# The output projection by groups of token tiles, with kept weights and an early residual load

## The reference

```python
D_MODEL, D_FF, SEQ, DEC_BATCH, DEC_SEQ = 1024, 2816, 512, 8, 8

def trunk_layer(x, ...):
    z = rmsnorm(x, g_mix_pre)
    q, kc, vc, ks, vs, kw, vw, g_nsa, u, g_mrg = mixer_inputs(z, w_in)
    o_attn, win_state = attend(q, g_nsa, kc, vc, ks, vs, kw, vw)
    o_conv, conv_state = conformer_conv(u, conv_hist, conv_w, conv_b, conv_ln_g, conv_ln_b)
    h = (g_mrg[:, :, 0] * (o_attn @ w_attn_out) + g_mrg[:, :, 1] * (o_conv @ w_conv_out)) @ w_out
    x = x + rmsnorm(h, g_mix_post)
    f, ffn_state = conv_ffn(rmsnorm(x, g_ffn_pre), ffn_hist, w_up, ffn_conv_w, ffn_conv_b, w_down)
    x = x + rmsnorm(f, g_ffn_post)
    return x, kv_rows, win_state, conv_state, ffn_state
```

## Time and profile before

| | us |
|---|---|
| median of 3 executions | 1005.52 (1005.27 to 1006.03) |
| the profiled execution | 1006.05 |
| its span, first to last instruction | 1004.4 |
| PE busy in it | 950.4 (95%) |
| DVE busy | 575.2 (57%) |
| ACT busy | 399.6 (40%) |
| POOL busy | 208.4 (21%) |

### The profile page before, as it was taken

How to read it: one execution, slowest core, us unless ns; L and a number is a source line. 1 busy time by engine, 2 the same in 40 slices (tenths; PEclk the granted TensorE clock), 3 DMA queues, 4 the chain that set the end, 5 groups by cost and what they waited for, 6 DMA issues and landing times.

```text
span 1004.4 us, 17775 instructions
## 1 busy us (share of the span) xinstructions
PE 950.4 (95%) x6757; PEld 859.9 (86%) x6757; DVE 575.2 (57%) x1083; ACT 399.6 (40%) x734; POOL 208.4 (21%) x274
## 2 busy tenths in 40 slices
PE   4999999996999999899995999999999999999995
PEld 2899999996888878799774999999999997777774
DVE  4448688997565664567146466666666664113114
ACT  6211162644354434522136355555555552312112
POOL 6443242444232323022100011111111111000000
PEclk9999999997999999999995899999999999999998
DMA  7655532331100001122720222222222222131212
GB/s 215 148 178 187 128 87 78 95 85 43 51 23 2 23 22 39 47 63 85 213 84 0 63 84 84 84 84 84 84 84 84 84 84 84 63 98 65 84 63 95
DMA packets 110753, 84.05 MB, mean 84 GB/s; under 512 B 12962, under 2 KB 97834, under 8 KB 110632
## 3 DMA queue, kind: packets, MB, share of 16 engines
q1 hardware_dynamic: 104368, 65.64, 22.7%
q0 software_dynamic: 3904, 14.66, 5.2%
q10 hardware_dynamic: 2426, 2.98, 1.0%
HBM read 78.19 MB, written 7.18 MB: 85 GB/s over the span
## 4 chain that ended last, share of the span: by engine, by line
PE 88%; DVE 3%; ACT 3%; issue 2%; DMA 2%; POOL 1%; POOLq 0%; ACTq 0%; DVEq 0%
PE ps L1466 24%; PE ps L1467 24%; PE ps L1468 24%; PE ps L1498 2%; PE ps L1750 2%; PE ps L1727 2%; PE ps L1533 2%; DMA page<-in_state_kv_win_dram 2%; PE ps L1687 1%; DVE yc L1146 1%; PE ps L1690 1%; PE ps L1584 1%; PE ps L1693 1%; PE ps L1746 1%; POOL page L595 1%
## 5 line engine op out<-in xcount | busy, mean ns | idle before, releaser
L1466 PE MATMUL ps<-zh,wh 128*128 128x288 f32 (+1 forms) x1264 | 383.1, 303 | 2.1 <-DVE zl L1399 2.0
L1467 PE MATMUL ps<-zl,wh 128*128 128x288 f32 (+1 forms) x1264 | 374.4, 296 | 0.0
L1468 PE MATMUL ps<-zh,wl 128*128 128x288 f32 (+1 forms) x1264 | 374.4, 296 | 0.0
L1466 PEld LDWEIGHTS ps<-zh,wh 128*128 128x128 f32 (+1 forms) x1264 | 238.1, 188 | 4.4 <-issue 2.7
L1467 PEld LDWEIGHTS ps<-zl,wh 128*128 128x128 f32 (+1 forms) x1264 | 238.3, 189 | 0.5
L1468 PEld LDWEIGHTS ps<-zh,wl 128*128 128x128 f32 (+1 forms) x1264 | 237.9, 188 | 0.5
L1077 DVE TENSOR_TENSOR wl<-raw,wh 128x1024 fp32r<-128x1024 f32 (+1 forms) x73 | 95.4, 1306 | 203.9 <-ACT wh L734 203.7
L734 ACT CAST wh<-raw 128x1024 fp32r<-128x1024 f32 (+1 forms) x73 | 76.0, 1041 | 314.0 <-PE ps L1468 299.0
L1146 DVE SCALAR_TENSOR_TENSOR yc<-ext,par,yc 128x512 f32<-128x512 f32 (+1 forms) x180 | 115.9, 712 | 0.0
L1034 ACT CAST wh<-raw 128x1024 fp32r<-128x1024 f32 x44 | 46.1, 1049 | 139.4 <-PE ps L1468 139.4
L695 POOL TENSOR_TENSOR hs<-cv 128x512 f32<-128x512 f32 x22 | 28.5, 1297 | 325.2 <-DVE cv L1432 325.2
(11 more groups left out here) (260 smaller groups left out, 1324.9 us busy)
## 6 DMA issues: line engine op xcount, KB each, us to landing
raw<-in_w_up_dram SPq DMA_DIRECT2D x44, 512.0 KB, 3.8
raw<-in_w_in_dram SPq DMA_DIRECT2D x30, 512.0 KB, 3.9
raw<-in_w_down_dram SPq DMA_DIRECT2D x22, 512.0 KB, 3.6
page<-in_cache_kv_dram POOLq DMA_DIRECT2D x16, 256.0 KB, 3.0
raw<-in_w_out_dram SPq DMA_DIRECT2D x8, 512.0 KB, 3.5
x<-in_x_prompt_dram SPq DMA_DIRECT2D x4, 512.0 KB, 5.4
page<-in_state_kv_win_dram POOLq DMA_DIRECT2D x16, 128.0 KB, 3.0
raw<-in_w_in_dram SPq DMA_DIRECT2D x8, 256.0 KB, 3.5
```

The costliest lines, as they stand in the source:

```text
L1466: nc.tensor.matmul(out, ah, bh, start=start, stop=False)
L1467: nc.tensor.matmul(out, ah, bl, start=False, stop=False)
L1468: return nc.tensor.matmul(out, al, bh, start=False, stop=stop)
```

## The change

It touches the stretch from the merge to the first turn of `w_up`.

- `w_out` is computed by groups of token tiles: tiles 0, 1 and 2 together over all eight slots, then tile 3 over all eight, then tile 4. For that the eight slots are kept: slots 0 and 1 in the ring, 2 to 7 in places of their own (`wo1` to `wo4`), so that their high parts no longer wait for PE. The order of the slots is now by channel pair and then by half.
- A tile's norm, residual and second norm are made per tile with 1024 columns at a time (`square_out`, `scaled_out`, `add_out`, `square_x1`, `norm_x1`). `norm_x1` multiplies by `gffn`, a broadcast copy of `g_ffn_pre`, so the split into `z2` is a plain copy and subtraction.
- Each tile is transposed on its own (`turn_z2`), between the matmuls of the tiles behind it. `z2` is laid out by halves of 288 rows, and the first turn of `w_up` is taken out of the loop: both tiles' first halves, then the last transposes, then the second halves.
- POOL issues the loads of `x1` and `gffn` at the start of the merge, ahead of its adds, and `gpost` and `sf` after the merge.

```diff
@@ SP
-            for half in range(2):
-                for kc in range(KT // 2):
-                    s = S_OUT + half * (KT // 2) + kc
+            for kc in range(KT // 2):
+                for half in range(2):
+                    s = S_OUT + 2 * kc + half
                     ring_free(s)
@@ POOL
+            pool.wait_ge(c_step, 2 * CT)
+            pool.wait_ge(m_attn, 1)
+            for i in range(TT):
+                src = x_prompt[0, i * P:(i + 1) * P, :] if i < 4 else xs_v
+                pool.dma_start(x1[0:ROWS[i], i, :], src).then_inc(x1_in, 16)
+            pool.dma_start(gffn[:, :], g_ffn_pre[0].partition_broadcast(P)).then_inc(gf_in, 16)
+
             for m in range(KT):
                 pool.wait_ge(m_mul, 2 * m + 2)
...
@@ ACT
-            for kc in range(KT // 2):
-                hi(S_OUT + kc + 2)
+            for st in range(2, 8):
+                s = S_OUT + st
+                act.wait_ge(raw_in[s % 2], raw_value(s))
+                act.wait_ge(slot_used, S_MRG)
+                nc.scalar.copy(out_w(st)[0], raw[:, s % 2, :]).then_inc(hi_done, 1)
...
+            def z2_high(n):
+
+                i, src, high, _ = z2_piece(n)
+                act.wait_ge(z2_full, i + 1)
+                if n < 3:
+                    act.wait_ge(slot_used, S_OUT + 4)
+                else:
+                    act.wait_ge(o_tile, TT)
+                if n == 3:
+                    act.wait_ge(z2_ok, 3)
+                nc.scalar.copy(high, src).then_inc(z2_hi, 1)
+
+            for t in range(6):
+                if t < 3:
+                    square_out(t)
+                if 1 <= t < 4:
+                    root_out(t - 1)
+                if 2 <= t < 5:
+                    square_x1(t - 2)
                 if t >= 3:
...
+                    root_x1(t - 3)
+            square_out(3)
+            root_out(3)
+            square_x1(3)
+            root_x1(3)
+            for n in range(3):
+                z2_high(n)
+            hi(S_UP)
             hi(S_UP + 1)
+            square_out(4)
+            z2_high(3)
+            root_out(4)
+            z2_high(4)
+            square_x1(4)
+            root_x1(4)
+            z2_high(5)
@@ DVE
+            scaled_out(3)
+            dve.wait_ge(sf_t, 1)
...
+            add_out(3)
+            mean_x1(3)
+            norm_x1(3)
+            for n in range(3):
+                z2_low(n)
+            lo(S_UP)
             lo(S_UP + 1)
+            scaled_out(4)
+            z2_low(3)
+            add_out(4)
+            z2_low(4)
+            mean_x1(4)
+            norm_x1(4)
+            z2_low(5)
@@ PE
+            for kc in range(KT // 2):
+                pe.wait_ge(m_ok, 2 * kc + 2 + AHEAD)
+                for half in range(2):
+                    pe.wait_ge(lo_done, S_OUT + 2 * kc + half + 1)
+                    for i in range(3):
+                        if kc == 0 and i == 2:
+                            pe.wait_ge(m_mul, 2 * KT)
+                        mm = out_mm(i, kc, half)
+                        if kc == KT // 2 - 1 and half == 1:
+                            mm.then_inc(o_tile, 1)
+            for kc in range(KT // 2):
+                for half in range(2):
+                    mm = out_mm(3, kc, half)
+            mm.then_inc(o_tile, 1)
             pe.wait_ge(sf_in, 16)
+            pe.wait_ge(o_ev, 2)
             for t in range(2 * FT):
...
+            turn_z2(0)
+            pe.wait_ge(o_ev, 3)
+            for kc in range(KT // 2):
+                for half in range(2):
+                    mm = out_mm(4, kc, half, kc in (1, 2))
+                if kc == 0:
+                    pe.wait_ge(sf_ok, 1)
+                    turn_z2(1)
+                if kc == 1:
+                    pe.wait_ge(o_ev, 4)
+                    turn_z2(2)
+            mm.then_inc(o_tile, 1)
+            pe.wait_ge(z2_ok, 2)
+            turn_z2(3)
+            pe.wait_ge(lo_done, S_UP + 1)
+            pe.wait_ge(z2_ok, 3)
+            tile(0, S_UP % 2, 0, KT, z2, halves=(0,))
+            pe.wait_ge(lo_done, S_UP + 2)
+            pe.wait_ge(z2_ok, 5)
+            tile(1, (S_UP + 1) % 2, 0, KT, z2, halves=(0,))
+            turn_z2(4)
+            pe.wait_ge(z2_ok, 6)
+            tile(0, S_UP % 2, 0, KT, z2, halves=(1,)).then_inc(slot_used, 1)
+            tile(1, (S_UP + 1) % 2, 0, KT, z2, halves=(1,)).then_inc(slot_used, 1)
+            with pe.Fori(1, FT) as i:
...
```

More of the change, by code:

```diff
@@ L245, in build_layer @@
         sf = at("sf", [2 * DB, 2 * FF], F32, C)
-        gpost = at("gpost", [P, D], F32, C + 2 * FF)
-        junk = at("junk", [P, TT, D], F32, A)
+        z2 = at("z2", [P, 2, 2, KT, HALF], F32R, A)
+        wo1 = at("wo1", [P, 2, 2, 1024], F32R, A)
+        wo2 = at("wo2", [P, 2, 2, 1024], F32R, A + 2 * KT * HALF)
+        wo3 = at("wo3", [P, 3, 1024], F32R, FV + TT * D)
+        wo4 = at("wo4", [P, 1024], F32R, E)
+        gpost = at("gpost", [P, D], F32, J - 1536)
+        gffn = at("gffn", [P, D], F32, J - 512)
+        assert FV + TT * D + 3 * 1024 <= I and J - 512 + D <= K - TT * D and C + 2 * FF <= E
         x1 = at("x1", [P, TT, D], F32, K - TT * D)
@@ L1020, in _, with square_out @@
[L1020 to L1023, removed]
-            hi(S_UP + 1)
+            def square_out(i):
+                act.wait_ge(o_tile, i + 1)
+                m = ROWS[i]
+                nc.scalar.activation(hb[0:m, i, :], out_ps(i), ACT.Square, accum_out=ss[0:m, i:i + 1]).then_inc(o_sq, 1)
@@ L1326, in _ @@
                     .then_inc(m_ok, 1)
-            for kc in range(KT // 2):
-                lo(S_OUT + kc + 2)
+            for st in range(2, 8):
+                s = S_OUT + st
+                dve.wait_ge(hi_done, s + 1)
+                high, low = out_w(st)
+                nc.vector.tensor_tensor(low, raw[:, s % 2, :], high.bitcast(F32), ALU.subtract).then_inc(lo_done, 1)
             def gained(i, half, sq, out, gain, done):
@@ new lines, in norm_x1, with z2_low @@
+            def norm_x1(i):
+                dve.wait_ge(rs3, i + 1)
+                m = ROWS[i]
+                nc.vector.scalar_tensor_tensor(hb[0:m, i, :], x1[0:m, i, :], rstd[0:m, i:i + 1], gffn[0:m, :],
+                                               ALU.mult, ALU.mult).then_inc(xn2, 1)
+            def z2_low(n):
+                _, src, high, low = z2_piece(n)
+                dve.wait_ge(z2_hi, n + 1)
+                nc.vector.tensor_tensor(low, src, high.bitcast(F32), ALU.subtract).then_inc(z2_ok, 1)
@@ L1397, in _ @@
[L1397 to L1402 removed]
+            for t in range(6):
+                if t < 3:
+                    scaled_out(t)
+                if 1 <= t < 4:
+                    add_out(t - 1)
+                if 2 <= t < 5:
+                    mean_x1(t - 2)
+                if t >= 3:
+                    norm_x1(t - 3)
@@ L1478, in tile @@
                             w = (view[0][:, k, :], view[1][:, k, :])
-                        last = three(pair(q, h * HALF, (h + 1) * HALF, m), w,
-                                     (src[0][:, k, cols], src[1][:, k, cols]), k == 0, k == kn - 1)
+                        last = three(pair(q, h * HALF, (h + 1) * HALF, m), w, a, k == 0, k == kn - 1)
                 return last
@@ L1881, in _, with out_mm, turn_z2 @@
             pe.wait_ge(m_mul, 2 * KT - 2)
-            token_major(S_OUT, KT, (mh, ml), m_ok, (m_mul, 2 * KT), o_ev, o_tile, lambda half, kc: None)
+            def out_mm(i, kc, half, used=False):
+                w = [v.rearrange("p (k n) -> p k n", n=512) for v in out_w(2 * kc + half)]
+                for kk in range(2):
+                    k = 2 * kc + kk
+                    mm = three(out_ps(i)[:, half * 512:(half + 1) * 512],
+                               (mh[:, k, i * P:i * P + ROWS[i]], ml[:, k, i * P:i * P + ROWS[i]]),
+                               (w[0][:, kk, :], w[1][:, kk, :]), k == 0, k == KT - 1)
+                    if used:
+                        mm.then_inc(slot_used, 1)
+                return mm
+            def turn_z2(i):
+                pe.wait_ge(xn2, i + 1)
+                for k in range(KT):
+                    mm = nc.tensor.transpose(z2_ps(i)[:, k, :], hb[0:ROWS[i], i, k * P:(k + 1) * P],
+                                             ident[0:ROWS[i], 0:ROWS[i]])
+                mm.then_inc(z2_full, 1)
+            for kc in range(KT // 2):
[12 more added lines that the diff above has]
+            mm.then_inc(o_tile, 1)
             pe.wait_ge(sf_in, 16)
+            pe.wait_ge(o_ev, 2)
             for t in range(2 * FT):
```

143 lines of the change are left out of this document (69 added, 74 removed).

## The result

| kernel | median, us | runs | lowest to highest | ratio to before |
|---|---|---|---|---|
| before | 1006.28 | 15 | 1004.3 to 1007.7 | 1 |
| changed | 993.75 | 15 | 991.8 to 1001.7 | 0.9889 [0.9876, 0.9903] |

The account below looks back on a forecast made before the run. PE was taken to wait between `w_out` and `w_up`, transposing in step with ACT and DVE at 1.2 GHz. -16.2 us of path plus 1.6 for one clock fall, -14.6, on 1005.52 gave 991.0 us; range 988.4 to 996.5.

Parts of the forecast that it names:

- The path to the turn's end: First `w_out` matmul to end of `w_up`'s first turn: 551.9 against 568.1, 16.2 us less before any clock fall.
- Tiles 0 to 3 end at 517.1: PE in `w_out`: the 192 matmuls of the first four token tiles end at 517.1 us, without waits.
- close: 0 taken, up to 9: Fourth `w_out` slot, due at 485.7, loaded beside `gpost`: 0 taken, up to 9 us if it lands in 15.3.
- Runs, tile 4, and the chain behind it: Transposes, tile 4's matmuls and norm chain up to 545.5 us, leaving PE idle 2.3 and 1.6 us.
- run 3: PE's run of eight transposes for token tile 3, behind tile 4's end at 533.6 us; predicted to end at 534.5.
- One fall, 1.5 to 1.6 us: Granted clock falls once, behind the small `sf` (past-row) transposes, for 3.4 us, costing 1.5 to 1.6 us; chance 0.41.
- The page's rule: Skill ties matmul-rate drops to idle gaps between bursts; by it no fall, 989.3 us; the no-fall rival had chance 0.25.
- The loads in the merge, 0 taken: `x1` and `gffn` beside the merge's weights: fifth load lands near 442, PE needs it at 448.1; 0 taken.
- Behind it the loop is the same in both kernels.: Behind `w_up`'s first turn PE fills the loop in both kernels, so what is won before is won at the end.
- no longer 12.8 us: Sign of being wrong: turns of the loop behind the first turn of `w_up` that are no longer 12.8 us.
- late load: Rival: a load comes 2 to 9 us late, in the merge or at the fourth `w_out` slot; 993 to 1000, chance 0.12.
- two or three falls: Rival: further clock falls, such as behind the idle 2.3 us after tile 4, 1.5 us each; 992.5 to 994, chance 0.16.

Follow-up runs that it names:

- experiment 2: Changed kernel with the loads of `gpost` and `sf` held until the last `w_out` slot is split; 994.62 us, ratio to before 0.9892.
- Experiment 4: Changed kernel with the 44 small past-row transposes moved from between `w_out`'s groups into PE's two waits, 22 in each; 990.92 us, ratio to before 0.9850.
- experiment 8: Changed kernel with the turns of tiles 0 to 2 moved from between tile 4's quarters to behind `w_out`; 997.84 us, ratio to before 0.9931.
- Experiment 6: Changed kernel with the 44 small past-row transposes run twice in their place, writing the same values; 1001.04 us, ratio to before 0.9953.
- Experiment 3: Changed kernel with the `x1` and `gffn` loads put back after the merge, beside `w_out`'s slots; 1004.17 us, ratio to before 0.9981.
- 10: Changed kernel with later `gpost` and `sf` loads and unread 512-column matmuls in PE's two waits; 992.23 us, ratio to before 0.9867.
- 7: Changed kernel with unread matmuls of 512 columns, 8 and 6, in PE's two waits; 994.85 us, ratio to before 0.9885.
- experiment 12: Experiment 5's kernel with `z2` laid out so that a chunk's high and low halves stand side by side; 988.78 us, ratio to before 0.9833.
- experiment 5: Changed kernel with both later `gpost` and `sf` loads and past-row transposes in PE's two waits; 988.73 us, ratio to before 0.9837.

## Why the prediction was right

**The path to the turn's end.** Predicted 16.2 us less without a fall and 14.6 with one; measured 13.1 with one (568.40 to 555.28). By its steps:

- *Tiles 0 to 3 end at 517.1.* They ended 1.8 later, at 518.9. This is the term that was mis-sized: "close: 0 taken, up to 9" for the fourth `w_out` slot. It landed in 8.15 us, between the two rows named (3.5 and 15.3), and cost 1.7 to 2.2 (experiment 2 takes it away). PE waiting in `w_out` for a low part of the weights is one of the prediction's own signs of being wrong; here it marks this term, small enough to leave the range unhurt.
- *Runs, tile 4, and the chain behind it.* From run 3 (predicted 533.6) to the last wait's end (545.5) 11.9 us were predicted, and 11.6 came (535.46 to 547.07). The waits were put at 2.3 and 1.6 and show as 1.91 and 1.40, with the releasers named. Experiment 4 shows that the chain of the fifth tile ends them, experiment 8 that the interleaved turns hide 2.7 us.
- *One fall, 1.5 to 1.6 us.* One came, of 3.4 us, but behind the second wait and not behind the past rows, where I had put it. Experiment 6 shows that the small transposes can bring a fall by themselves; experiments 2, 3 and 10 have one behind them and the first run of eight, in some executions and not in others. 7 and 10 show the other place without a fall once wide matmuls fill the wait. So the size was right, and the count was right by luck: the fall that the sum priced didn't come in this execution, and another came.
- *The page's rule.* The Trainium skill (TensorE: Matmul & The Clock Gate, "Why this matters for your kernels") names idle gaps between bursts as what brings a drop. Experiment 2's trace shows a drop without one: PE full from 474.2, the level at 0.52 from 521.3.

**The loads in the merge, 0 taken.** Right: the merge ended at 473.2 (473.4 before), and the fifth load's high part started within 0.3 us of its old time. Experiment 3 shows what the other place costs, 8 to 10 us of median (1004.17 against 996.22 and 993.75).

**"Behind it the loop is the same in both kernels."** Wrong, by 6.40 - 6.36 over 42 tiles, 1.7 us; the layout of `z2`, a part of the change that the prediction put at nothing, made it (experiment 12). Its sign for this, turns "no longer 12.8 us", could not catch it: a turn is 12.80 now and was 12.72. Luck hid it: the profile of before had a low stretch at the start of `w_down` (838 to 842), that of the changed kernel had none there, and the two cancel. From the turn's end to the end of the span both profiles take 436.1 us.

**The sum.** The profiled execution was to gain 14.6 us and gained 13.1. The 1.5 lie ahead of the turn's end: the changed kernel reached it at 555.28 where 551.9 and one fall make 553.5, 1.8 late, the same as behind tile 3; and before ended its turn at 568.4 where the working has 568.1. The medians lie 2.75 apart, 991.0 and 993.75. Beside these 1.5, 0.8 is the median of before, 1006.28 in 15 runs for 1005.52 in three; the 0.5 left is within the spread of the runs.

**The rivals.** In the profiles the late load came, just under its lower end of 2 us, in `w_out` and not in the merge, and the profile of the result had one fall in the tail. The median of 993.75 doesn't tell the cases apart: it lies in the band of two or three falls and in that of a late load. The chance of 0.12 for the late load was too small for a slot that the working itself called close.

## What to carry to other kernels

A slot that the working calls "close" beside named competitors should be priced between the rows, not at the better one, and the competitors moved behind it. In a tail that PE fills, look for work that nobody waits for (here 44 transposes) and put it into waits that a norm chain makes; it was worth 3 us of the path. When operands change place, compare the period of the untouched loop behind them, since 0.04 us a tile is a microsecond or two over the loop.

## What the runs showed of the hardware that I had not expected

- The granted clock can fall with PE never idle: behind 44 transposes of 16 columns and eight of 128, 0.52 over the next 3.4 us (experiment 2); 2.4 us into a run of 88 small ones (experiment 6). The same 44 were followed by no fall in five other executions (the changed kernel's three, 7 and 8).
- A wait's length alone doesn't tell whether a fall follows: behind 1.91 us none, behind 1.40 us one (the changed kernel), where a run of eight transposes stands just ahead of the shorter wait.
- The pitch of matmuls of 288 columns hangs on how the moving operand (`z2`, of which the columns stream through PE) lies in the on-chip memory: 6.40 us for 48 with high and low halves 9216 bytes apart and chunks every 1152 (experiment 5), 6.35 with the halves side by side and chunks every 2304 (experiment 12). Why, no run here shows.
- A 512 KB load of weights landed in 8.15 us beside 0.9 MB from another queue (the changed kernel), in 3.6 us when those loads came later (experiment 2).
